# Constant products on TensorE around the norms, and a convolution norm moved into the attention, in a three-layer transformer kernel

## Chip, cores and metric

One core of one Trainium2 chip runs the whole program in one launch. The metric is the device time of one execution in microseconds; of the kernel before it is the median of three runs.

## The reference

512 tokens of width 1024 pass through two equal layers (first block), then one different layer (second block), all in float32.

- First block, twice: `x = LN(a*x + 0.5*swiglu(x))`, hidden width 2816; `x = LN(a*x + mix)`; the same FFN form again with other weights. The mixer projects `x` to queries and keys of two attentions: one with latent queries and keys (8 heads, 64 + 32 rotary columns), one sparse attention (8 heads, 2 key groups, window, selected and compressed keys). Rotary tables are `cos` and `sin` of position. Two sigmoid-gated projections are added and projected once more.
- Second block: `x = x + mix(rms(x)) @ w_out`, then a mixture of 16 experts with top-2 routing. The mix is the concatenation of three parts:

```
o_gla  = gated linear attention (4 heads of 64), rms norm per head, times silu(out_gate)
y      = causal depthwise conv (width 31) of a * sigmoid(g)          # 256 channels
yn     = group norm of y over 64 channels, * gain + bias;  o_conv = yn * sigmoid(yn)
o_diff = (softmax(q1 k1^T) - lam * softmax(q2 k2^T)) v, rms norm per head of 128, gain
mix    = concat(o_gla, o_conv, o_diff);  x = x + mix @ w_out
```

## The kernel before

**Layout.** Activations lie transposed: 8 tiles of 128 features by 512 tokens (`xa`). Each float32 product is made of three in a faster format: an operand is split into a high and a low part (`xhi`, `xlo`; `whi`, `wlo`), and TensorE adds high x low, low x high and high x high in one bank. A weight block is 128 output features: 24 matmuls of 128x512. SyncE loads it into `raw` (two slots), ScalarE rounds it to `whi` (line 569), GpSimd subtracts for `wlo` (line 2631); `whi`/`wlo` have four slots, freed in order by `w_free`. Each engine runs its instructions in program order; the order is written out by hand, with semaphores between engines. `sync_point` (line 393) is a barrier between stages: TensorE and ScalarE raise `at_sync`, VectorE waits for both, clears the local semaphores and lets them go.

**First block.** `pe_ffn` (line 483) computes the FFN. Its first two tiles run interleaved, following the norm tile by tile (`pe_first_pair`, line 465): for each `k` four matmuls on `xhi[k]`, two on `xlo[k]`. The down projection has 8 output tiles of two blocks of 11 (66 matmuls). VectorE adds a finished tile to the residual (line 675) and accumulates sums in `zs` and squares in `sq_sum`; the last tile's sums come separately. `pe_stats` (line 516) turns these into per-token statistics with matmuls of one column (line 520, `sums`), then spreads the reciprocal roots over a bank (`pe_spread`, line 551, transposes). `dve_stats` (line 729) computes in between. Then comes `sync_point`, then the norm: VectorE, ScalarE (`xhi`) and GpSimd (`xlo`) tile by tile. After the FFN follow `pe_mixer` (line 1035), a barrier, `pe_mixer_out` (line 1152: MLA units with gate products as filler, projections), `pe_stats`, and the second FFN. Between the two layers VectorE frees the banks for the next FFN only after its norm.

At the start of the mixer ScalarE issues five DMAs (lines 1191 to 1197): two of the rotary tables `rope`, two of `w1`, one of `vbd`. All add to `cmp_dma`. `rope` lies in memory that the FFN's `hlo` occupies. VectorE waits for all five (line 1316) before tile 0's rotation (`rotate`, line 1305: multiply, shuffle at line 1309, which frees the bank). TensorE waits for them at the compression.

**Second block.** `pe_squares` (line 536) sums squares by pairs of tiles for the first norm. `pe_second` (line 1591) runs 19 input tiles with the linear attention's levels and the convolution taps (60 on VectorE) beside them, then 32 attention units (`pe_units_whole`, line 793; 4 heads x 2 maps x 4 query tiles; 128 to 512 keys). Unit `u` on TensorE: filler (`pe_late`), scores of `u`, transposes of unit `u - 2`, values of `u - 3`. `act_units` and `dve_units` call `act_late` and `dve_late` after each unit in the same way. The filler is four late projection tiles, six matmuls a unit over units 0 to 15 (24 in all for each), then the rest of the linear attention; the output gates are made of `Exp` (ScalarE, units 20, 21), add and reciprocal (VectorE, unit 22). `finish_dif` (line 2226) combines eight groups of four units.

After the last unit: VectorE squares and reduces the attention's output (lines 2252, 2254) for the per-head norm, ScalarE takes the root, VectorE scales all of it (line 2262), TensorE transposes 16 blocks (line 1651). The conv norm runs beside it: means by `blk64` (line 1642), subtraction (2258), squares (1978), variance (1646), root (1981), reciprocal of 128x1024 (2265), gain, bias, sigmoid (1986), product (2276). `split_mix` (line 2103) writes each mix tile's high and low part; heads follow one by one. `mix_ready` counts tiles. TensorE waits for all eight, then runs the eight tiles of `w_out`, one after the other in two banks, with `pe_pair_sums` for the next norm among them. Router, gather and 23 expert blocks follow.

## Time and profile before

| | us |
|---|---|
| median of 3 runs (3226.43 to 3226.77) | 3226.52 |
| profiled execution | 3226.44 |
| its span | 3224.6 |
| TensorE busy | 2927.3 (91%) |
| VectorE busy | 1526.1 (47%) |
| ScalarE busy | 1216.3 (38%) |
| GpSimd busy | 1167.2 (36%) |

The mean granted TensorE clock is 0.949 of full speed. Times in the trace count from the first instruction. Engines are PE (TensorE matmul), PEld (its weight loads), DVE (VectorE), ACT (ScalarE), POOL (GpSimd), SP (SyncE). In a timeline a row is a start, a duration, engine, line and operation, and in brackets how long the engine was idle before and which engine's work ended that. A matmul of two fp32 operands is two records.

### The profile page before, as it was taken

What the parts mean: (1) busy time and instruction counts of PE and PEld (TensorE: products, weight loads), DVE (VectorE), ACT (ScalarE), POOL (GpSimd) and SP (SyncE); (2) the same over time, 40 slices, a digit from 0 to 9 for tenths busy, and PEclk for the clock granted to TensorE, in tenths of its full rate; (3) what the DMA queues carried; (4) which work ended last, traced back from release to release, by engine and by line L of the source; (5) the groups of instructions that cost most, each with busy time, mean ns of one, the idle gap of its engine ahead of it and who ended that gap; (6) DMA issues with size and microseconds to landing.
All of it is one profiled execution on the core that took longest, in us unless ns stands there. A gap on an engine that the chain in (4) does not pass through costs nothing.

```text
span 3224.6 us, 38218 instructions
## 1 busy us (share of the span) xinstructions
PE 2927.3 (91%) x13393; PEld 2335.0 (72%) x13393; DVE 1526.1 (47%) x2594; ACT 1216.3 (38%) x1854; POOL 1167.2 (36%) x602
## 2 busy tenths in 40 slices
PE   6999989988999998999989998999999797866997
PEld 5887777657778876887868756778878676655665
DVE  4441364445744314433154544663332577555665
ACT  3332233555343323333132465443332342424553
POOL 3444342421444443444443341244444342011221
PEclk9999999999999998999989999999999798978998
DMA  3333232202323331333232211323332121014996
GB/s 127 94 96 104 78 121 71 64 17 67 123 85 97 97 99 61 91 98 106 94 104 79 86 30 33 110 76 105 92 105 96 36 79 46 20 65 150 358 354 208
DMA packets 118547, 324.19 MB, mean 101 GB/s; under 512 B 12432, under 2 KB 48656, under 8 KB 117904
## 3 DMA queue, kind: packets, MB, share of 16 engines
q1 hardware_dynamic: 108992, 305.17, 29.6%
q10 hardware_dynamic: 2800, 8.91, 0.7%
q0 software_dynamic: 6624, 8.41, 0.7%
q8 instruction: 77, 1.26, 0.2%
q14 instruction: 54, 0.44, 0.0%
HBM read 313.52 MB, written 24.64 MB: 105 GB/s over the span
## 4 chain that ended last, share of the span: by engine, by line
PE 63%; issue 15%; DVE 10%; POOL 7%; ACT 4%; DMA 2%; POOLq 0%; DVEq 0%; ACTq 0%; SPq 0%; another core or an unknown queue 0%
PE ps L417 14%; PE ps L418 14%; PE ps L420 14%; POOL wlo L2631 6%; PE ps L452 3%; PE ps L1910 2%; PE ps L929 2%; PE ps L1896 1%; PE ps L1898 1%; PE ps L1897 1%; DVE cacc L2178 1%; PE ps L827 1%; PE ps L1739 1%; PE ps L1882 1%; ACT xhi L646 1%
## 5 line engine op out<-in xcount | busy, mean ns | idle before, releaser
L2631 POOL TENSOR_TENSOR wlo<-raw,whi 128x1024 fp32r<-128x1024 f32 (+1 forms) x368 | 953.4, 2592 | 1580.2 <-ACT whi L569 1580.2
L417 PE MATMUL ps<-xlo,whi 128*128 128x512 f32 x1736 | 683.7, 394 | 40.8 <-DVE xlo L2107 19.2
L569 ACT ACTIVATE whi<-raw 128x1024 fp32r<-128x1024 f32 (+1 forms) x368 | 409.1, 1112 | 820.8 <-PE ps L420 779.6
L418 PE MATMUL ps<-xhi,wlo 128*128 128x512 f32 x1736 | 680.5, 392 | 0.0
L420 PE MATMUL ps<-xhi,whi 128*128 128x512 f32 x1736 | 428.7, 389 | 0.0
L417 PEld LDWEIGHTS ps<-xlo,whi 128*128 128x128 f32 x1736 | 329.6, 190 | 113.1 <-issue 21.7
L418 PEld LDWEIGHTS ps<-xhi,wlo 128*128 128x128 f32 x1736 | 329.2, 190 | 67.9
L420 PEld LDWEIGHTS ps<-xhi,whi 128*128 128x128 f32 x1736 | 325.9, 188 | 67.7
L417 PE MATMUL ps<-hlo,whi 128*128 128x512 f32 x704 | 281.4, 400 | 10.0 <-DVE hlo L664 10.0
L418 PE MATMUL ps<-hhi,wlo 128*128 128x512 f32 x704 | 279.3, 397 | 0.0
L675 DVE SCALAR_TENSOR_TENSOR xa<-ps,xa 128x512 f32<-128x512 f32 x48 | 33.1, 690 | 405.5 <-PE ps L420 405.5
L659 DVE TENSOR_TENSOR sg<-sg,ps 128x512 f32<-128x512 f32 x88 | 60.6, 688 | 346.8 <-PE ps L420 346.1
L664 DVE TENSOR_TENSOR hlo<-sg,hhi 128x512 f32 x88 | 213.2, 2422 | 10.8
L592 ACT ACTIVATE sg<-ps 128x512 f32<-128x512 f32 x88 | 52.8, 600 | 334.0 <-PE ps L420 312.0
L420 PE MATMUL ps<-hhi,whi 128*128 128x512 f32 x704 | 171.5, 391 | 0.0
L417 PEld LDWEIGHTS ps<-hlo,whi 128*128 128x128 f32 x704 | 134.5, 191 | 42.1 <-issue 12.7
L656 DVE TENSOR_TENSOR sg<-sg,ps 128x512 f32<-128x512 f32 x88 | 60.5, 688 | 215.6 <-ACT sg L592 215.6
L418 PEld LDWEIGHTS ps<-hhi,wlo 128*128 128x128 f32 x704 | 134.5, 191 | 30.5 <-issue 1.0
L420 PEld LDWEIGHTS ps<-hhi,whi 128*128 128x128 f32 x704 | 132.2, 188 | 29.0
L2431 DVE TENSOR_TENSOR mlo<-mraw,mhi 128x2048 fp32r<-128x2048 f32 x46 | 103.3, 2288 | 49.8 <-ACT mhi L2060 49.6
L452 PE MATMUL ps<-xlo,whi 128*128 128x512 f32 x256 | 116.5, 455 | 8.7 <-DVEq L397 4.6
L452 PE MATMUL ps<-xhi,wlo 128*128 128x512 f32 x256 | 108.6, 424 | 0.0
(569 smaller groups left out, 4729.6 us busy)
## 6 DMA issues: line engine op xcount, KB each, us to landing
raw<-in_gu SPq DMA_DIRECT2D x176, 512.0 KB, 3.6
raw<-in_mix SPq DMA_DIRECT2D x96, 512.0 KB, 3.7
mraw<-in_w SPq DMA_DIRECT2D x23, 2048.0 KB, 12.3
raw<-in_dn SPq DMA_DIRECT2D x64, 704.0 KB, 4.0
mdraw<-in_w SPq DMA_DIRECT2D x23, 1024.0 KB, 13.4
raw<-in_w SPq DMA_DIRECT2D x32, 512.0 KB, 3.6
gate_rows<-tails SPq DMA_DIRECT2D x32, 256.0 KB, 4.3
sgmn<-gate_rows SPq DMA_DIRECT2D x16, 512.0 KB, 4.3
```

Of the source, the lines that this page charges most:

```text
L417: nc.tensor.matmul(out, whi[:, slot, cols], rlo, start=first and t == 0, stop=False)
L418: nc.tensor.matmul(out, wlo[:, slot, cols], rhi, start=False, stop=False)
L420: ins = nc.tensor.matmul(out, whi[:, slot, kk * P:kk * P + P], rhi, start=False, stop=last and t == n - 1)
L452: ins = nc.tensor.matmul(out, w[:, slot, t * P:t * P + P], x[:, t, :], start=k == 0, stop=k == 3 * KT - 1)
L569: nc.scalar.activation(whi[:, s, 0:n], raw[:, r, 0:n], ACT.Copy).then_inc(hi_done, 1)
L656: nc.vector.tensor_tensor(sg[:, j, :], sg[:, j, :], ps[0][:], ALU.mult).then_inc(S["tile_free"], 1)
L659: nc.vector.tensor_tensor(sg[:, j, :], sg[:, j, :], ps[1][:], ALU.mult).then_inc(S["tile_free"], 1)
L664: nc.vector.tensor_tensor(hlo[:, bass.ds(i * 2 + j, 1), :], sg[:, j:j + 1, :], hhi[:, bass.ds(i * 2 + j, 1), :].bitcast(F32), ALU.subtract ...
L929: ins = nc.tensor.matmul(bank[:], v_keys[:, br, kt, :], p_group[G % 2][:, kt, :, :].rearrange("p j q -> p (j q)"), start=br == 0 and kt == ...
L1910: ins = nc.tensor.matmul(ps[2 + half][:].rearrange("p (n c) -> p n c", n=4), hT[b % 2][:, j, :], mdraw[b % 3][:, 4 * half:4 * half + 4, j, ...
L2431: nc.vector.tensor_tensor(mlo[b % 2][:, :, k], mraw[b % 2][:, :, k], mhi[b % 2][:, :, k].bitcast(F32), ALU.subtract).then_inc(m_lo, 1)
L2631: nc.gpsimd.tensor_tensor(wlo[:, s, 0:n], raw[:, r, 0:n], whi[:, s, 0:n].bitcast(F32), ALU.subtract).then_inc(w_ready, 1)
```

## The change

1. `rope` gets a semaphore of its own and is issued by ScalarE before the barrier that ends the first FFN; `cmp_dma` thresholds fall by 32.
2. The sums of `zs` and `sq_sum` move out of `pe_stats` into the last tile: between its two blocks in the FFN, between its low passes and its high pass in the mixer.
3. `pe_idle(n)` issues `n` products of the identity and a 128x256 constant into a bank that nothing reads. They stand in `sync_point` after TensorE's increment (5 after each `pe_stats`, 8 between mixer and mixer output, 9 and 2 in the second block), in `pe_stats` (2 and 1), in `pe_squares` (24, then 1 after each of four pairs), after the last two pair sums (2 and 1) and before the experts' gather (10).
4. The conv norm's statistics, roots, reciprocal (eight pieces), gain and bias move into units 0 to 15 of the attention; the late tiles run eight matmuls a unit over units 4 to 15; conv and output gates use one `Sigmoid` group at unit 20. `finish_dif` reduces squares by group; heads are scaled one by one; `w_out` tiles 0 to 3 run together in four banks, by mix tile.

```diff
+    def pe_idle(n, bank=None):
+        for _ in range(n):
+            nc.tensor.matmul((bank or ps[5])[:, 0:256], ident, c("maskc")[:, 0:256], start=True, stop=True)
@@ sync_point(eng, who, idle=0)
             eng.sem_inc(S["at_sync"], 1)
+            pe_idle(idle)
             eng.wait_ge(go, 1)
@@ products(..., between=None)
             nc.tensor.matmul(out, wlo[:, slot, cols], rhi, start=False, stop=False)
+        if between:
+            between()
@@ down(i, mm), in pe_ffn
+                if b == 0 and mm == KT - 1:
+                    pe_early_sums(pe)
@@
+    def pe_early_sums(pe):
         pe.wait_ge(S["own2"], 11)
         sums(ps[4], 0, zs[:])
         pe.wait_ge(S["pair_ready"], 6)
         sums(ps[4], 4, sq_sum).then_inc(S["pair_used"], 1)
+    def pe_stats(pe, t0):
+        pe_idle(2)
         pe.wait_ge(S["tile_free"], t0 + 2 + KT)
         sums(ps[2], 0, xa[:, KT - 1, :]).then_inc(S["pair_used"], 1)
         pe.wait_ge(S["squared"], KT)
         sums(ps[3], 0, sq_one).then_inc(S["pair_used"], 1)
+        pe_idle(1)
...
@@ pe_mixer_out
+                       between=(lambda: pe_early_sums(pe)) if j == KT - 1 else None)
@@ dve_mixer
-        dve.wait_ge(S["cmp_dma"], 80)
+        dve.wait_ge(rope_in, L * 32 + 32)
@@ pe_second, after the units
-        pe.wait_ge(S["own_cq"], 1)
-        for k in range(2):
-            ins = nc.tensor.matmul(ps[k][:], c("blk64"), cacc[:, k, :], start=True, stop=True)
...
+        for b in range(4):
+            pe.wait_ge(w_ready, B2 * G_LAYER + (G2_OUT + b + 1 + 2))
+        pe.wait_ge(S["mix_ready"], 4)
+        for k in (2, 3):
+            pe_four_tiles(pe, k)
         for h in range(4):
+            pe.wait_ge(S["gl_ready"], h + 1)
             for qt in range(QT):
                 ins = nc.tensor.transpose(ps[4 + h][:, qt * P:(qt + 1) * P], o_dif[:, qt, h * P:(h + 1) * P], ident)
             ins.then_inc(S["aux_ready"], 1)
+            if 1 <= h <= 2:
+                pe_four_tiles(pe, h - 1)
+        for k in range(4, KT):
+            pe.wait_ge(S["mix_ready"], k + 1)
+            pe_four_tiles(pe, k)
+        for j in range(4, KT):
+            pe_x_block(pe, B2, G2_OUT, 0, j, j % 4, j - 1)
...
@@ pe_four_tiles(pe, k): for b in range(4), ps[b] += three products of mix tile k
@@ pe_late
+        if u == 0:
+            for k in range(2):
+                ins = nc.tensor.matmul(ps[k][:], c("blk64"), cacc[:, k, :], start=True, stop=True)
+            ins.then_inc(S["stat_ready"], 1)
+        if u == 2:
+            for k in range(2):
+                pe.wait_ge(S["sq_ready"], k + 1)
+                nc.tensor.matmul(ps[k][:], c("blk64"), rs2[:, k, :], start=True, stop=True).then_inc(S["stat_used"], 1)
+        n, k0 = divmod(u - LATE_AT, LATE_UNITS)      # LATE_AT, LATE_UNITS = 4, 3; before 0, 4
+                if n < 2:
+                    pe.wait_ge(S["std_ready"], n + 1)
@@ act_late
+            for k in range(2):                        # u == 1
+                act.wait_ge(S["norm_dve"], k + 1)
+                nc.scalar.activation(rs2[:, k, :], cacc[:, k, :], ACT.Square).then_inc(S["sq_ready"], 1)
+        if u == 3:
+            for k in range(2):
+                act.wait_ge(S["stat_used"], k + 1)
+                nc.scalar.activation(rs2[:, k, :], ps[k][:], ACT.Sqrt, bias=eps_ap(RMS_EPS)).then_inc(S["std_ready"], 1)
+        if u == OG_AT:
+                nc.scalar.activation(og_sig[:, half, :], og[half][:], ACT.Sigmoid).then_inc(S["og_exp"], 1)
+            nc.scalar.activation(conv_sig[:], cacc[:], ACT.Sigmoid).then_inc(S["sig_ready"], 1)
@@ dve_late
-            own.link(nc.vector.tensor_scalar(og_sig[:], og_sig[:], 1.0, None, ALU.add))
-            own.link(nc.vector.reciprocal(og_sig[:], og_sig[:]))
+        if u == 1: ...                                # cacc -= mean, two 128x512
+        if 5 <= u < 13:
+            r = rs2[:, (u - 5) // 4, (u - 5) % 4 * P:(u - 5) % 4 * P + P]
+            own.link(nc.vector.reciprocal(r, r))
+        if u == 13: ...                               # gain;  u == 14: bias
+        if u == OG_AT + 3: ...                        # cacc *= conv_sig, 128x1024
+        if u in (OG_AT + 5, OG_AT + 7): ...           # split_mix of conv tiles 2 and 3
@@ finish_dif
+            for h in range(2):
+                own.link(nc.vector.tensor_tensor_reduce(sg[:, 0, 256 + P * h:256 + P * h + P], o[:, h, :], o[:, h, :], 1.0,
+                                                       0.0, ALU.mult, ALU.add, rt3[:, r:r + 1]))
@@ act, first layer loop, after act_ffn and act_root
+            for k in range(2):
+                act.dma_start(rope[:, 2 * k:2 * k + 2, :], ...).then_inc(rope_in, 16)
             sync_point(act, "act")
```

## Rows read from the trace of the kernel before

**Rows 1.** TensorE's waits, all: who for whom, total us, times, longest
```profile
PE ps L417 <- DVE xlo L2107: 19.2, 1, 19.2
PE ps L417 <- DVE sg L1309: 17.0, 4, 8.4
PE ps L547 <- DVE squares L769: 16.3, 3, 14.6
```
**Rows 2.** Stretches, second block: length, busy us by engine, clock, DMA share, GB/s
```profile
2724.00:2764.00 40.00, 39.72 (x204) 29.46 (x204) 12.26 (x59) 19.24 (x52) 9.52 (x4) 1.00 0.18 53
2764.00:2784.00 20.00, 16.95 (x100) 12.84 (x100) 10.68 (x38) 11.36 (x29) 0.00 (x0) 1.00 0.00 1
2784.00:2803.00 19.00, 11.41 (x51) 10.15 (x51) 11.12 (x15) 2.46 (x6) 0.00 (x0) 0.64 0.00 1
2803.00:2826.00 23.00, 20.87 (x141) 16.77 (x140) 17.64 (x43) 13.57 (x26) 0.00 (x0) 1.00 0.00 1
2826.00:2864.00 38.00, 10.24 (x27) 5.17 (x25) 31.04 (x34) 8.85 (x11) 2.43 (x1) 0.54 0.05 14
2864.00:2913.00 49.00, 48.67 (x213) 40.37 (x213) 7.36 (x12) 9.17 (x12) 12.35 (x5) 0.94 0.29 97
```
**Rows 3.** Short stretches at either clock: PE, PEld, DVE, ACT, POOL, clock
```profile
404.30:409.10 4.80, 4.80 (x11) 3.41 (x12) 4.80 (x8) 4.80 (x8) 4.12 (x4) 0.50 0.00 0
409.60:417.50 7.90, 7.90 (x36) 6.54 (x35) 2.99 (x5) 6.70 (x9) 7.21 (x6) 1.00 0.50 177
425.40:429.40 4.00, 3.98 (x9) 3.13 (x10) 3.86 (x3) 0.14 (x1) 2.60 (x1) 0.50 0.02 9
709.60:713.80 4.20, 4.15 (x15) 3.67 (x16) 1.61 (x7) 2.28 (x6) 0.00 (x0) 0.58 0.00 0
1969.90:1976.90 7.00, 7.00 (x22) 5.92 (x23) 3.38 (x12) 4.59 (x11) 0.00 (x0) 0.56 0.00 0
2563.90:2577.60 13.70, 13.70 (x48) 10.96 (x48) 11.18 (x21) 5.25 (x8) 7.55 (x5) 0.78 0.01 1
```
**Rows 4.** Timeline, start of the mixer, layer 0
```profile
417.76 0.59 ACT L1202 ACTIVATE g_t<-ps 24x512 f32<-24x512 f32 x1 [0.55 <-PE ps L479]
...
423.93 0.69 DVE L1308 TENSOR_TENSOR k_pe<-ps,rope 32x512 f32<-32x512 f32 x1 [11.20 <-DMA vbd<-in_zero]
...
424.55 0.72 DVE L1309 STREAM_SHUFFLE sg<-ps 32x512 f32<-32x512 f32 x1
...
425.42 0.77 PE L417 MATMUL ps<-xlo,whi 128*128 128x512 f32 x1 [7.47 <-DVE sg L1309]
```
**Rows 5.** Timeline, end of the first FFN, layer 0
```profile
394.89 0.95 PE L520 MATMUL ps<-con,zs 128*128 128x1 f32 x8
...
395.09 0.69 DVE L675 SCALAR_TENSOR_TENSOR xa<-ps,xa 128x512 f32<-128x512 f32 x1 [10.88 <-PE ps L420]
...
396.59 1.03 PE L520 MATMUL ps<-con,xa 128*128 128x1 f32 x8
...
404.26 0.79 PE L475 MATMUL ps<-xhi,whi 128*128 128x512 f32 x1 [2.92 <-ACT xhi L646]
```
**Rows 6.** Timeline, end of the mixer, layer 0
```profile
886.30 1.05 PE L520 MATMUL ps<-con,zs 128*128 128x1 f32 x8 [0.23 <-DVE zs L719]
```
**Rows 7.** Timeline, attention of the second block; last, a line of groups
```profile
2776.69 1.56 PE L1753 MATMUL ps<-vT,k_rows 128*128 128x256 f32 x6 [2.30 <-ACT vT L1789]
...
2784.37 6.55 DVE L1807 RECIPROCAL og_sig<-og_sig 128x1024 f32<-128x1024 f32 x1
...
2816.23 1.28 ACT L1796 ACT_TABLE_LOAD   x1
...
2817.53 0.31 ACT L1796 ACTIVATE small<-small 128x16 f32<-128x16 f32 x1
...
L861 DVE CUSTOM_DVE_ANT_0 s_sb<-ps,con 128x128 f32<-128x128 f32 (+3 forms) x66 | 32.4, 491 | 84.5 <-PE ps L808 83.6
```
**Rows 8.** Timeline, before the MLA units, layer 0
```profile
705.77 0.47 PE L452 MATMUL ps<-xlo,whi 128*128 128x512 f32 x1 [2.30 <-DVEq L397]
```

More of the change, by code:

```diff
@@ L402, in sync_point, with products @@
             eng.sem_inc(S["at_sync"], 1)
+            pe_idle(idle)
             eng.wait_ge(go, 1)
             eng.sem_clear(go)
-    def products(out, parts, first=True, last=True, ready=None):
+    def products(out, parts, first=True, last=True, ready=None, between=None):
         n = len(parts)
@@ L422, in products, with pe_x_block @@
         return ins
-    def pe_x_block(pe, L, g, i, j, bank, free, ver=None, x=(xhi, xlo), ready=None):
+    def pe_x_block(pe, L, g, i, j, bank, free, ver=None, x=(xhi, xlo), ready=None, between=None):
         pe.wait_ge(w_ready, L * G_LAYER + i * 4 + (g + j + 1 + 2))
@@ L514, in pe_shift, with sums @@
         nc.tensor.matmul(ps[2][:], c("ones"), zs[:], start=True, stop=True).then_inc(S["stat_ready"], 1)
-    def pe_stats(pe, t0):
-        def sums(bank, c0, x):
-            for qt in range(QT):
-                ins = nc.tensor.matmul(bank[:, c0 + qt:c0 + qt + 1], x[:, qt * P:(qt + 1) * P], c("ones")[:, 0:1],
-                                       start=True, stop=True)
-            return ins
+    def sums(bank, c0, x):
+        for qt in range(QT):
+            ins = nc.tensor.matmul(bank[:, c0 + qt:c0 + qt + 1], x[:, qt * P:(qt + 1) * P], c("ones")[:, 0:1],
+                                   start=True, stop=True)
+        return ins
+    def pe_early_sums(pe):
         pe.wait_ge(S["own2"], 11)
@@ L1790, in act_late @@
                                      ACT.Copy).then_inc(S["v_rows"], 1)
-            if u == OG_AT + half:
+        if u == OG_AT:
+            for half in range(2):
                 act.wait_ge(S["late_out"], 3 + half)
-                nc.scalar.activation(og_sig[:, half, :], og[half][:], ACT.Exp, scale=-1.0).then_inc(S["og_exp"], 1)
+                nc.scalar.activation(og_sig[:, half, :], og[half][:], ACT.Sigmoid).then_inc(S["og_exp"], 1)
+            act.wait_ge(S["own_cq"], 1)
+            nc.scalar.activation(conv_sig[:], cacc[:], ACT.Sigmoid).then_inc(S["sig_ready"], 1)
         if u == GLA_AT + 4:
@@ L2250, in dve_second @@
-        flat = o_dif[:].rearrange("p q (h v) -> p (q h) v", v=P)
-        sq = sqd[:].rearrange("p q (h v) -> p (q h) v", v=P)
-        own.link(nc.vector.tensor_tensor(sq, flat, flat, ALU.mult))
-        own.wait()
-        nc.vector.tensor_reduce(rt2, sq, AX_X, ALU.add).then_inc(S["gel_ready"], 1)
-        dve.wait_ge(S["stat_ready"], 1)
-        for k in range(2):
-            nc.vector.tensor_tensor(cacc[:, k, :], cacc[:, k, :], ps[k][:], ALU.subtract).then_inc(S["norm_dve"], 1)
-        dve.wait_ge(S["gel_ready"], 2)
@@ L2260, in dve_second @@
-        own.link(nc.vector.reciprocal(rt2, rt2))
-        own.wait()
-        nc.vector.tensor_tensor(flat, flat, rt2.unsqueeze(2).broadcast_to([P, 16, P]),
-                                ALU.mult).then_inc(S["gl_ready"], 1)
-        dve.wait_ge(S["std_ready"], 2)
-        own.link(nc.vector.reciprocal(rs2[:], rs2[:]))
-        own.wait()
-        for k in range(2):
-            own.link(nc.vector.scalar_tensor_tensor(out=cacc[:, k, :], in0=cacc[:, k, :], scalar=p2("cng", k),
-                                                   in1=rs2[:, k, :], op0=ALU.mult, op1=ALU.mult))
@@ L2270, in dve_second, with scaled @@
-        own.wait()
-        for k in range(2):
-            own.link(nc.vector.tensor_scalar(cacc[:, k, :], cacc[:, k, :], p2("cnb", k), None, ALU.add))
-        own.wait()
-        dve.sem_inc(S["own_cq"], 1)
-        dve.wait_ge(S["sig_ready"], 1)
-        own.link(nc.vector.tensor_tensor(cacc[:], cacc[:], rs2[:], ALU.mult))
-        own.wait()
-        for k in range(2):
-            split_mix(dve, own, 2 + k, cacc[:, k, :])
+        dve.sem_inc(S["gel_ready"], 1)
+        def scaled(h):
+            o = o_dif[:, :, h * P:(h + 1) * P]
+            r = rt3.rearrange("p (q h) -> p q h", h=4)[:, :, h:h + 1].broadcast_to([P, QT, P])
+            nc.vector.tensor_tensor(o, o, r, ALU.mult).then_inc(S["gl_ready"], 1)
@@ L2280, in dve_second @@
+        dve.wait_ge(S["gel_ready"], 2)
+        own.link(nc.vector.reciprocal(rt3, rt3))
+        own.wait()
+        scaled(0)
+        scaled(1)
         for h in range(4):
@@ L2831, in _ @@
             act_root(act, LN_EPS)
+            for k in range(2):
+                act.dma_start(rope[:, 2 * k:2 * k + 2, :], d["rope"].rearrange("k p t -> p k t")
+                              [:, 2 * k:2 * k + 2, :]).then_inc(rope_in, 16)
             sync_point(act, "act")
```

133 lines of the change are left out of this document (75 added, 58 removed).

## The prediction

> **What bounds the kernel now.** I read the totals first: TensorE is busy 91% of the span, so a microsecond is won only where TensorE stands still or runs at the low clock. The list of TensorE's waits then says where it stands still [rows 1]: 19.2 us once, ahead of the second block's output projection; two stretches of about 8 us behind a VectorE shuffle (line 1309); 14.6 us ahead of the second block's first norm. The table of stretches shows what stands around the longest [rows 2]: from 2826 to 2864 TensorE is busy 10.24 of 38 us and VectorE 31.04, so VectorE's serial chain of sub-layer norms is the bound there; from 2784 to 2803 TensorE has 11.41 of 19 us at a mean clock of 0.64. The table of short stretches gives the price of the clock [rows 3]: after a norm the granted clock is 0.50 (1.2 GHz) and 11 records take 4.80 us, 0.436 each; later it is 1.00 (2.4 GHz) and 36 take 7.90, 0.219 each. The reader is to see that a slow stretch costs only where TensorE is the bound, and then half of its length.
>
> **Part 1, rope tables early.** The first rotation of each layer waits 11.20 us for DMAs, and what it waits for last is the fifth transfer in ScalarE's queue, two weight tables of 1 MB among the five [rows 4]. Tile 2 of the mixer needs the bank that this rotation frees, so TensorE stands 7.47 us in layer 0 and 8.4 in layer 1 [rows 1, 4]. With the tables issued before the norm and only they awaited, the wait is over long before 412. What is late next is the ordinary chain: gate sigmoid 0.59, rotation 0.69, shuffle 0.72, and the handoffs, some 2.3 us for each layer. ScalarE's two issues stand beside VectorE's two scalings after the statistics (1.4 us, two passes at L675's 0.69 [rows 5]) and are hidden; uncovered they would cost under 1 us each layer. The compression waits for its weights much later. Gain: 7.5 + 8.4 - 2 x 2.3 = 11.3 us. The slow 4.0 us after the wait (9 records, clock 0.50) [rows 3] go as well, 2 us each, unless the new 2.3 us gap drops the clock; I take half. **-13.3**, bounds -15 and -9.
>
> **Part 2, early sums.** Now the sixteen one-column products for `zs` and `sq_sum` follow the last tile (from 394.89), beside VectorE's add (395.09, 0.69), and the sums of `xa` start at 396.59 [rows 5]. Moved into the last tile, they cost TensorE the same 1.9 us, but nothing covers the add any more: it now ends 0.95 us after a tile that itself ends 1.9 us later, where before the sums of `xa` started 1.55 us after the tile. The chain is 1.9 + 0.95 - 1.55 = 1.3 later; I take 1.15, since the `squared` wait hides a little. Four FFN boundaries: +4.6. In the mixer it is worse: there the sums stand behind the low passes of one 5.5 us tile, which end at 884.1, while `zs` is ready only at 886.3 [rows 6], so TensorE stalls 2.2 us with eight matmuls behind the wait. Two boundaries at 2.8: +5.6. Bounds for the part: 0 (if the products slip between matmuls) and +12.
>
> **Part 3, idle products.** No row shows a 128x256 constant product; the nearest is L1753, fp32 with 256 columns, six records (three products) in 1.56 us at full clock [rows 7]: 0.47 to 0.52 us each, about twice that at the low one. Five fill 2.4 of the 2.92 us ahead of the next norm's first tile [rows 5]; 5 + 24 take 14 us of the 14.6 [rows 1]; nine 4.3 of 4.8. All fit if the clock is full when they start, and it is, since dense tiles precede. What they buy, with each after-norm pair of tiles held at 48 records: TensorE needs 11 us, but the low half arrives every 1.3 us and paces it at 12.2, against 13.7 now. So a pair gains 1.1 to 1.5 us, not the 2.4 that the clock alone gives: -5.5 for four. The broadcast transposes gain 0.45 at each of six: -2.7. Between the two layers TensorE waits 14 us with five idles, so that restart stays slow: 0. The second block's squares gain 2.1 in their four-step ping-pong and its pair 1.6 (clock 0.78 over 13.7 us [rows 3]): -3.7. With part 2: **-1.7**, bounds -6 and +14. The upper one: clock falls regardless, nothing is gained, each idle group overhangs its gap by 1 us.
>
> The eight idles before the MLA units fill the wait of 2.30 us [rows 8] and the 2.7 behind it; the gate feed slips 1.2 us inside that gap, at no cost. Behind it 4.2 us run at clock 0.58 in layer 0 and 7.0 at 0.56 in layer 1 [rows 3], TensorE busy throughout: half of each, 5.6. **-5**, bounds -6 and +2. The remaining idles (router, gather) sit in gaps and win about **-1**.
>
> **Part 4, second block.** Tail: from the last attention product (2826.2) to the last tile of the projection (2912.6) pass 86.4 us. After: norm statistics are gathered unit by unit, the conv result is ready, and TensorE starts on rows 2 and 3 of the first four tiles (24 matmuls, 5.5 us) while VectorE scales head 0. I walked the heads: each costs VectorE about 2.6 us (scaling, gain, split in two) and each group of 12 matmuls costs TensorE 2.7, so TensorE never waits. It needs 192 matmuls at 0.228 (213 records in 48.67 us [rows 2]) 43.8, 16 transposes 1.8, sums 1.9, and one gap: slots of the first four tiles come free together at the end, so tile 4 waits for ScalarE's and GpSimd's conversion, 1.75. Together 49.2: -37.2. Bounds -40 and -30.
>
> Attention: the statistics of the conv norm stand at units 0 and 2, and late tile 0 waits at unit 4 for ScalarE's roots. With TensorE in order, squares (after VectorE's two subtractions) hold it till 2730.3 and the roots with their table load till 2736.9, where unit 4 now begins at 2732.9: +4.0. The late tiles lose four units of overlap: 24 of 96 matmuls move onto units 4 to 15, +5.5. The two holes of 3.5 and 2.6 us may cost clock: +2. Against it, VectorE's add and reciprocal of the output gates (6.55 us at 2784.37 [rows 7]), which hold the softmax chain and then the clock through the recurrent products (0.64 [rows 2]), become one sigmoid: unit 25's scores come 11.9 us earlier, less 1.4 for ScalarE's 4.9 us of sigmoids and tables at unit 20: -10.5. The cost of the same reciprocal in eight pieces is hidden: VectorE has 12.26 of 40 us in those units. In units 25 to 31 it has 17.64 of 23 us [rows 2]; two splits (under 1.4 each, two passes of 0.69) and four reductions (nearest form, L861, 0.49 [rows 7]) make it the bound: +2.5. Sum **+3.5**, bounds -6 and +14.
>
> ScalarE here takes two switch pairs more. The row: a load takes 1.28 and its activation begins 0.02 later, 2816.23 to 2817.53 [rows 7]; I used that. The Trainium skill, page "ScalarE: Activation LUTs", section "What ACT_TABLE_LOAD costs", adds a drain of about 1.38 us to each switch, 2.66 in all. By that rule the four loads would cost 5.5 us more on ScalarE and the sum would be 3177; the row shows no such time behind the load or ahead of it.
>
> **Sum.** -13.3 - 1.7 - 5 - 1 - 37.2 + 3.5 = -54.7. The profiled execution took 3226.44 us (span 3224.6); so 3171.7. The median of the three runs, 3226.52, is 0.1 above it.
>
> **Rivals.**
> 1. The attention becomes latency-bound: VectorE's and ScalarE's queued norm work delays the softmax chain in every unit. For: two engines in order, ten inserted waits. Against: VectorE is busy under a third of units 0 to 15 [rows 2]. It would take part 4's attention to its +14, and the tail to -32: 3171.7 + 10.5 + 5 = 3187.
> 2. The clock does not hold: low activity around the one-column products drops it as now, and idles run at double length. For: the clock falls now while TensorE is still issuing such products. Against: dense idles stand before, between and behind them. Parts 2 and 3 at their upper ends, +14 and +2 in place of -1.7 and -5, give 3194; with half of the places failing, 3183.
> 3. The clock gives more: stretches that now fall by chance of a 2.5 us gap do not fall. For: the falls at gaps of that size come and go in this trace. 3159.
> 4. The tables' drain as a mechanism of this kernel: ScalarE stands 1.4 us more at each of four switches in the attention, all reaching TensorE: 3177. Only the page speaks for it.
> 5. Slower: idle products are real work in TensorE's order, 116 of them. If most waits that they should fill have gone and the clock stays low, each costs its full 1 us: +116 against -55 - 3. It decides from 55 of them exposed at the low clock, where the sum's gain is spent; at 70, 3171.7 + 70 = 3242. Against: the waits of 14.6 [rows 1], 2.92 [rows 5] and 2.30 us [rows 8] stand in the rows and nothing in the change removes them.
> 6. The change does not do what it says: the conv norm in the attention saves nothing since head norms alone hold VectorE as long. They are four of 2.6 us against TensorE's 2.7, so this needs them doubled: tail -15, 3194.
>
> **How the numbers follow.** Forecast 0.50; rival 1 0.14; 2 0.12; 3 0.12; 4 0.04; 5 0.03; 6 0.05. The likeliest is 3171.7. Its own range, from half of each part's bounds added as independent, is 3163 to 3180. The range reaches to rivals 1, 2 and 3 and leaves out 5 and 6: 3154 to 3190. Faster by over 0.2% (6.5 us, about what a measurement of this kernel tells from none) in every case but 5 and a part of 6: 0.96; within 0.2% 0.015; slower 0.025.
>
> **What would show it.** Right: the 19.2 us wait is gone, TensorE is busy over 90% from the attention's end, with one gap near 1.8 us ahead of tile 4; the shuffle waits are near 2 us; a stall of 2 us stands inside the last output tile of both mixers; the clock is 1.00 through five norms and low between the layers; TensorE has two holes in units 0 to 4. Wrong: the clock at 0.50 behind the idles; VectorE ahead of TensorE's waits in the projection; a saving outside 37 to 73 us.

## The result, and the profile after

The changed kernel took 3193.02 us (median of four, 3181.23 to 3199.03), 0.9887 of the kernel before, 95% interval 0.9872 to 0.9902: 1.1% faster, where 3171.7 was forecast and the range ended at 3190. The sign held, the size did not: 33.5 us instead of 54.7, by medians. Ten times of the changed kernel in two sets lie between 3181.2 and 3199.6; the lowest two have a granted clock of 0.970 and 0.971 and the highest two 0.964 and 0.965. The kernel before, near 3226.5 in its first times, spread as widely when it was run eleven times beside the experiments (3220.8 to 3236.7). So differences of a few microseconds are read from traces below, and from medians only above some 8 us.

The profiled execution took 3188.26 us (span 3186.2). Its page, the line of busy times and the granted clock by slices:

```profile
PE 2961.5 (93%) x13625; PEld 2361.4 (74%) x13625; DVE 1525.9 (48%) x2632; ACT 1217.9 (38%) x1856; POOL 1173.6 (37%) x602
...
PEclk9999999999999999999999999999999998999998
```

TensorE's waits in the second block, from 2640 to 2890 us (who waits for whom, total, times, longest), answer to [rows 1] and [rows 2]: the 19.2 us behind the split is gone; new are the two waits at L1768 and L1783, in the first units of the attention. The first line, in the router, stood before too, with 15.2 us.

```profile
PE ps L1938 <- DVE k_wide L2281: 18.3, 1, 18.3
...
PE ps L1768 <- ACT rs L1826: 3.7, 1, 3.7
PE ps L1783 <- ACT rs L1830: 2.5, 1, 2.5
...
PE ps L425 <- POOL wlo L2684: 1.6, 1, 1.6
```

Three stretches of the same block: length, busy us of PE, PEld, DVE, ACT, POOL, clock, DMA share, GB/s. The second and third are the output stage: TensorE has 56.9 of 59 us, where [rows 2] had 10.24 of 38. The first is the price at the attention's start: TensorE is busy all the time, at 0.50.

```profile
2729.00:2739.00 10.00, 9.60 (x26) 6.96 (x27) 0.51 (x3) 2.86 (x6) 0.00 (x0) 0.50 0.00 0
...
2822.00:2864.00 42.00, 40.37 (x208) 34.27 (x208) 23.96 (x46) 10.24 (x16) 9.97 (x4) 0.97 0.14 38
2864.00:2881.00 17.00, 16.53 (x86) 13.89 (x85) 3.78 (x6) 3.48 (x5) 2.40 (x1) 1.00 0.50 187
```

**The account.** Each product of TensorE in one trace has its like in the other. The difference of their start times is taken ahead of a step and behind it; by how much it moved is what the step cost. So the whole difference divides (us, against the trace of the kernel before; the last column is a second trace of the same changed kernel):

```
step                                        forecast   first trace  second trace
rotary tables, two layers                     -13.3       -13.6        -11.8
mixer's end to second FFN, layer 0             +1.0        +4.0         +4.8
mixer's end to second FFN, layer 1             +1.0        +4.2         +2.8
first FFN's end to mixer, both layers          -1.4        -1.2         -1.3
FFN's end to next layer                        +0.7        +1.3         +1.3
FFN's end to the second block's tiles          -3.0        -1.7         -3.0
MLA units                                      -5          -4.6         -4.2
attention, from before it to its last product  +3.5       +12.2        +12.0
output stage                                  -37.2       -37.2        -37.2
all else (router, clock falls by chance)       -1          -1.6         -6.1
sum                                           -54.7       -38.2        -42.7
```

A row changes by 1.5 or 3 us where the clock fell once more or less. One row can change by much more, since it rests on a single trace of the kernel before: its attention, from its first product to its last, took 101.7 us there, and 110.5 in the trace of a kernel whose second block is the same ("Rotary tables alone" below). The mean granted clock over it was 0.93 in the one and 0.81 in the other. The changed kernel's 113.1, in both its traces, is 11.5 above the one and 2.7 above the other. So the +12 of that row is sure only against this one trace. The forecast's rows 2 to 6 are its -1.7, put where its terms belong: two mixers at 2.8, four FFN boundaries at 1.15, less the pairs', transposes' and squares' gains.

### The profile page after: what moved, and what is told of

It reads as the page before. It is cut to its first block, busy times and chain, and to the rows that moved or that the text cites. A ratio compares the mean times of both kernels' runs of the same rounds, so it can differ in the third digit from the quotient of the medians.

```text
span 3186.2 us, 38726 instructions
## 1 busy us (share of the span) xinstructions
PE 2961.5 (93%) x13625; PEld 2361.4 (74%) x13625; DVE 1525.9 (48%) x2632; ACT 1217.9 (38%) x1856; POOL 1173.6 (37%) x602
## 4 chain that ended last, share of the span: by engine, by line
PE 40%; issue 32%; POOL 14%; DVE 9%; ACT 3%; DMA 1%; POOLq 0%; SPq 0%; DVEq 0%; ACTq 0%; another core or an unknown queue 0%
POOL wlo L2684 13%; PE ps L430 6%; PE ps L425 6%; PE ps L426 6%; PE ps L462 3%; PE ps L1988 2%; PE ps L950 2%; PE ps L1974 1%; PE ps L1976 1%; PE ps L1975 1%; DVE cacc L2246 1%; PE ps L848 1%; PE ps L1783 1%; POOL xlo L808 1%; PE ps L1960 1%
## 5 line engine op out<-in xcount | busy, mean ns | idle before, releaser
L425 PE MATMUL ps<-xlo,whi 128*128 128x512 f32 x1704 | 668.0, 392 | 13.7 <-DVE sg L677 6.4
L426 PE MATMUL ps<-xhi,wlo 128*128 128x512 f32 x1704 | 665.0, 390 | 0.0
L430 PE MATMUL ps<-xhi,whi 128*128 128x512 f32 x1704 | 420.8, 389 | 0.0
L425 PEld LDWEIGHTS ps<-xlo,whi 128*128 128x128 f32 x1704 | 321.2, 189 | 84.9 <-POOL wlo L2684 11.4
L426 PEld LDWEIGHTS ps<-xhi,wlo 128*128 128x128 f32 x1704 | 321.1, 188 | 66.0
L685 DVE TENSOR_TENSOR hlo<-sg,hhi 128x512 f32 x88 | 213.1, 2422 | 10.8
L462 PE MATMUL ps<-xlo,whi 128*128 128x512 f32 x256 | 114.6, 448 | 4.1 <-DVE o_nsa L1463 4.1
L462 PE MATMUL ps<-xhi,wlo 128*128 128x512 f32 x256 | 106.5, 416 | 0.0
```

The source lines that it names most:

```text
L425: nc.tensor.matmul(out, whi[:, slot, cols], rlo, start=first and t == 0, stop=False)
L426: nc.tensor.matmul(out, wlo[:, slot, cols], rhi, start=False, stop=False)
L430: ins = nc.tensor.matmul(out, whi[:, slot, kk * P:kk * P + P], rhi, start=False, stop=last and t == n - 1)
L462: ins = nc.tensor.matmul(out, w[:, slot, t * P:t * P + P], x[:, t, :], start=k == 0, stop=k == 3 * KT - 1)
L685: nc.vector.tensor_tensor(hlo[:, bass.ds(i * 2 + j, 1), :], sg[:, j:j + 1, :], hhi[:, bass.ds(i * 2 + j, 1), :].bitcast(F32), ALU.subtract ...
```

## The experiments

**The changed kernel again.** No edit.

> The changed kernel once more, unedited, for a second trace and more times. Its four times so far spread from 3181 to 3199 us (granted clock 0.970 and 0.965), while the kernel before stays near 3226.5. Theory: the low-clock stretches fall differently from run to run, since the changed kernel leaves many gaps of 2 to 4 us that sometimes drop the clock; so the times spread again by over 10 us around 3190, a low time goes with a high granted clock, and work outside the low-clock stretches takes the same time as in the first trace. Rival: the spread was chance of the chip on that day; then five times lie within 3 us of each other.

3187.47 us (3183.61 to 3199.55). The theory held: the same spread, and a high clock with a low time. Its column stands above: the two traces of one kernel differ by clock falls, and by some 1.5 us in each of two down projections (see the end).

**The mixers' sums late.**

```diff
-                       between=(lambda: pe_early_sums(pe)) if j == KT - 1 else None)
+                       between=None)
...
-        pe_idle(2)
+        if not early:
+            pe_early_sums(pe)
+        else:
+            pe_idle(2)
```

> The early sums are undone in the two mixers alone (they follow the last tile again, and the two idle products ahead of them go); the four FFN boundaries keep theirs. Theory: in the last output tile of each mixer TensorE waits 2.02 us for the sum zs, which VectorE shares with GpSimd's weight work, and this stall also drops the clock, so that the eight high products after it take 3.65 us in place of 2.00; with the sums behind the tile both go, and the first norm product of each mixer comes 3 to 4 us earlier: 6 to 8 us in all, about 3186 against 3193. Rival 1: only the stall goes and the clock falls a little later instead, 4 us in all. Rival 2: the loss at the mixers comes from the restart behind the norm, not from the sums: within 1 us of the changed kernel.

The median, 3188.98 (3170.14 to 3192.48), shows no gain over the changed kernel's 3187.47. The profiled execution is the fastest of the five by 16 us, so what follows is read from single steps of its trace, not from its time. Mixer's end in the changed kernel, layer 0, TensorE's and VectorE's rows (start, us, line, tiles, count, idle before and its releaser):

```profile
874.65 2.15 DVE L740 TENSOR_TENSOR zs<-zs,xa 128x512 f32<-128x512 f32 x1
...
876.85 1.05 PE L531 MATMUL ps<-con,zs 128*128 128x1 f32 x8 [2.02 <-DVE zs L740]
877.76 1.04 PE L531 MATMUL ps<-con,sg 128*128 128x1 f32 x8
878.67 3.65 PE L430 MATMUL ps<-yhi,whi 128*128 128x512 f32 x8
...
890.40 0.50 PE L485 MATMUL ps<-xhi,whi 128*128 128x512 f32 x1 [1.18 <-ACT xhi L667]
```

and with the sums behind the tile:

```profile
876.41 2.00 PE L430 MATMUL ps<-yhi,whi 128*128 128x512 f32 x8
878.62 1.05 PE L531 MATMUL ps<-con,zs 128*128 128x1 f32 x8 [0.21 <-DVE zs L743]
...
887.85 0.58 PE L485 MATMUL ps<-xhi,whi 128*128 128x512 f32 x1
```

In the first, TensorE stands 2.02 us and the eight high products take 3.65 us instead of 2.00. The sums take their 1.8 us in either place, but behind the tile they cover VectorE's last add; here idle products (0.94 us) stand beside it instead, where only 0.21 were spent: 2.02 + 1.65 + 0.73 = 4.4. From the last low product to the sums of `xa` pass 8.65 to 10.21 us in all twelve such places of the six traces with the sums inside the tile, and 4.24 to 4.27 in every trace with the sums behind it, the kernel before among them. The larger values come where the clock falls among the sums already (the second group of them takes 1.85 us instead of 1.03 in layer 1 of the first trace). Against the kernel before, the step up to the norm's first tiles is now -1.0 us in layer 0 and -1.2 in layer 1 instead of the two traces' means of +4.4 and +3.5: 5.4 and 4.7 us won. The theory's 3 to 4 us for each mixer was too low, since it left out the add and the earlier falls.

Two things about the cause. The sum is late because the add to `zs` (L740) takes 2.15 us beside a GpSimd pass over weights; the same add takes 0.69 in the four FFNs, where no such pass runs beside it. And the one-column products alone don't bring the clock down: the same early sums, without a stall, stand between dense products at the four FFN boundaries, and in all 24 such places of the six traces they take 1.7 us and the clock stays. The first of them:

```profile
386.34 0.95 PE L531 MATMUL ps<-con,zs 128*128 128x1 f32 x8
387.15 1.03 PE L531 MATMUL ps<-con,sg 128*128 128x1 f32 x8
388.04 0.48 PE L425 MATMUL ps<-hlo,whi 128*128 128x512 f32 x1
```

Whether the stall would do it here without such products behind it is not shown: no run has it that way in this place, and behind the 2.0 us waits at tile 2 of the mixers, where none stand, the clock fell in some traces and not in others.

**No idle products.** `pe_idle` returns at once.

> All products on constants are taken out, nothing else. Theory: they work where a dense stretch precedes them and the gap is short: they won about 1.4 us at the first FFN boundary, some 4 us at the two starts of the MLA units and 1.7 us at the second block's first norm, and cost next to nothing where they win nothing; without them the kernel is 8 to 14 us slower, about 3203. Rival 1 (the forecast's size: 16 us of clock gains): 3209. Rival 2: the idle products are exposed or useless in most places: not slower than 3193.

3198.27 us (3185.77 to 3201.86), 10.8 above the changed kernel in the same set (5.3 above its first median), near the theory, though the intervals of the two ratios overlap (0.9877 to 0.9917, and 0.9862 to 0.9901). In its trace the MLA units of layer 1 gain nothing (0.1 us in place of -3.8 and -4.0), the second block's start nothing (in place of -1.7 and -3.0), the first FFN's end 0.1 (in place of -0.8). So the idle products do win in these places. Their sum, about 11 us where the forecast's terms together held 18, rests on the medians and is loose.

**One bank for the norm's statistics.** The sums go through bank 1 one at a time (units 0, 1, 3, 4); late tile 0 runs in bank 0 over units 0 to 3, the others from unit 6.

```diff
+        if u < 4:
+            return 0, 6 * u, 6
+        n, k0 = divmod(u - 6, 3)
+        return (n + 1, 8 * k0, 8) if u >= 6 else (-1, 1, 0)
...
+            nc.tensor.matmul(ps[1][:], c("blk64"), cacc[:, u, :], start=True, stop=True).then_inc(S["stat_ready"], 1)
```

> The statistics of the convolution's norm in the attention take one bank instead of two, one product at a time (units 0, 1, 3, 4), so that the first late projection tile runs in the other bank over units 0 to 3 as it did in the kernel before; the other three follow from unit 6 on, eight products a unit. The computation is the same. Theory: what made the attention's start 18 us worse than in the kernel before (the forecast had 11.5) is that TensorE has nothing to do over units 0 to 3 but wait for the squares (3.7 us) and the roots (2.5 us), that the clock falls there and stays low for 10 us, and that 24 products wait till unit 4; with late products between them both holes go and the attention ends 10 to 14 us earlier, about 3181. Rival 1: the softmax chain through VectorE and ScalarE, with the norm's work queued in it, sets the pace of every unit: at most 3 us are won. Rival 2: only the clock goes back, not the order: 5 us.

3188.39 us (3187.32 to 3194.93): the theory failed, nothing was won. The first units of the attention in the changed kernel, then two rows of this one, a wait of TensorE from 2764 to 2812 us and a stretch:

```profile
2714.93 1.98 PE L1763 MATMUL ps<-cacc,con 128*128 128x512 f32 x4 [1.87 <-DVEq L404]
...
2721.11 3.09 PE L1768 MATMUL ps<-rs,con 128*128 128x512 f32 x4 [3.71 <-ACT rs L1826]
...
2729.40 0.77 PE L1783 MATMUL ps<-xlo,whi 128*128 128x512 f32 x1 [2.46 <-ACT rs L1830]
```
```profile
PE ps L848 <- ACT pt L868: 4.1, 1, 4.1
```
```profile
2773.00:2804.00 31.00, 30.31 (x106) 24.15 (x107) 13.82 (x47) 15.06 (x32) 0.00 (x0) 0.51 0.03 13
```

The start did gain: unit 16's first score product comes 54.4 us after the attention's first product instead of 56.8. But holes of 1.5 and 3.1 us remained, with 17 us of low clock from the first of them on, and then the clock fell once more, at 2773, and stayed low for 30 us: units 22 to 24 took 3.37 us each, in the changed kernel 1.87, 3.40 and 1.87.

**Idle products in the two holes.**

```diff
         if u == 2:
+            pe_idle(7, ps[7])
             for k in range(2):
...
+        if u == 4:
+            pe_idle(5, ps[7])
```

> Idle products are added in the two places of the attention's start where TensorE waits: seven ahead of unit 2's wait for the squares (3.71 us), five ahead of unit 4's wait for the roots (2.46 us); one takes 0.46 us at the full clock in the changed kernel's trace. Theory: the low clock that begins in the first hole costs the squares' products 1.1 us (3.09 in place of 1.98) and units 2 to 6 some 5 us (unit 4 to 5 takes 7.74 and 5.08 where a unit with eight late products at the full clock takes 2.82); with the holes filled the clock stays, and unit 16 comes 5 to 6 us earlier after unit 0 than its 54.87 us. Rival 1: the clock falls in spite of the idle products: nothing is won, or 1 us lost where they overhang. Rival 2: ScalarE and VectorE hold units 2 to 6 anyway: under 2 us. In the time of the whole this is near what one set of rounds can tell, so the trace's units decide.

3179.38 us (3177.32 to 3183.34), 8.1 below the changed kernel's 3187.47, with intervals that overlap a little (0.9835 to 0.9874, and 0.9862 to 0.9901). The products that took 3.09 us, and the stretch behind them that ran at 0.50:

```profile
2716.12 1.98 PE L1769 MATMUL ps<-rs,con 128*128 128x512 f32 x4 [0.49 <-ACT rs L1829]
```
```profile
2718.00:2730.00 12.00, 11.40 (x56) 8.72 (x56) 2.91 (x13) 6.81 (x16) 0.00 (x0) 1.00 0.14 43
```

Unit 16 comes 48.98 us after unit 0 instead of 54.87: 5.9 us, as the theory had it. The effect goes on: the 10 us at 0.50 near the attention's end are down to some 3, and from its first product to its last pass 105.0 us instead of 113.1. The output stage then has a new gap of 1.27 us at its start and takes 50.6 us instead of 49.4. In three other traces with the holes unfilled ("All sums late", "Long idle" and the last experiment) the clock fell at other moments and unit 16 came 53.2 to 53.3 us after unit 0, so what the holes cost in clock is 4.3 us there.

**All sums late.** As the mixers' case, at the FFN boundaries too.

> The early sums are undone at all six boundaries (they follow the last tile again), and the two idle products ahead of the last tile's sums go with them; one idle stays ahead of the transposes. The run with only the mixers' sums late won 5.4 us at each mixer in its trace. Theory: at the mixers again 5 us each; at the four FFN boundaries, where the sums are ready in time and cost only their own 1.9 us uncovered, 1.2 us each, if the clock holds up to the norm: 15 us in all against the changed kernel's trace, 4 to 5 us better than with the mixers' alone. Rival: with the early sums' work gone from before and the idles gone from beside the last add, the clock falls around the one-column products at the FFN boundaries, the transposes take 1.97 us again in place of 1.09 and the first norm pair runs slow: worse by 1 to 2 us at each FFN boundary than the changed kernel.

3172.65 us (3169.45 to 3177.30), 14.8 below the changed kernel, and the intervals of the ratios don't overlap (0.9813 to 0.9847). The theory's 15 us came, but not in its places: at the FFN boundaries the trace shows -0.9, +1.3, -1.1 and -1.9 us, the changed kernel -0.8, +1.3, -0.4 and -1.7 to -3.0. The sums' 1.2 us were won and mostly given to the clock, by the rival's mechanism, though its loss of 1 to 2 us at each boundary did not come. The mixers' steps are won as before (4.27 and 4.26 us from the last low product to the sums of `xa`). Where the rest of the 14.8 us lies isn't shown: with the mixers' sums alone late the median was 3188.98, 16 us above this one, while the pair of kernels below that differ in the same way are 0.1 us apart. The transposes of the first one, here and in the changed kernel:

```profile
401.17 1.97 PE L573 MATMUL ps<-con,small 128*128 128x128 f32 x8
```
```profile
399.46 1.09 PE L575 MATMUL ps<-con,small 128*128 128x128 f32 x8 [0.32 <-DVE small L766]
```

**Rotary tables alone**, on the kernel before.

> The kernel before with the one edit that ScalarE issues the rotary tables ahead of the norm and VectorE waits for them alone. Theory: the wait of 7.5 and 8.4 us at tile 2 of each mixer becomes one of about 2 us, and the low clock behind it goes: 13 to 14 us, so 3213 against 3226.5, and in the trace the offset to the kernel before moves by 6 to 7.5 us between the norm and tile 3 of each mixer and nowhere else. Rival 1: the tables come late in their new place too, since they share the queue with the blocks of weights: under 8 us. Rival 2: the low clock of the norm's first pair now reaches further into the mixer and takes 2 us of each back: 10 us.

3211.92 us (3205.21 to 3218.89) against 3228.19 in the same set, ratio 0.9950 (0.9932 to 0.9968). In the trace the step is -7.6 us in layer 0 and -7.4 in layer 1, and the end -14.6. So the theory's steps came; its "nowhere else" did not. The offset moved by up to 5 us in other places too, where the code is that of before, and back by 8.8 in the attention. The wait that was 7.47 us [rows 4], and the stretch of the attention at the low clock that the trace of before doesn't have at this length:

```profile
419.04 0.47 PE L418 MATMUL ps<-xlo,whi 128*128 128x512 f32 x1 [1.98 <-DVE sg L1307]
```
```profile
2757.00:2794.00 37.00, 32.87 (x116) 26.34 (x115) 17.94 (x34) 7.98 (x19) 0.00 (x0) 0.50 0.00 1
```

**Long idle between the layers.**

```diff
-            sync_point(pe, "pe", 5)
+            sync_point(pe, "pe", 28)
```

> The changed kernel with 28 idle products in place of five between the layers, where TensorE waits 11 to 14 us for VectorE's norm, and 1 in place of 24 at the second block's start (the two follow each other, so that place keeps its number). Theory: at the restart between the layers the clock is 0.50 now and the first pair of tiles takes as long as before; with the wait filled it stays at 1.00, and the restart is 1.3 to 2.5 us earlier; nothing else moves. Rival 1: the idles run at the low clock from the start (they begin as it falls, at 1268 us), take 0.9 us each, overhang the wait by 10 us and the kernel is 10 us slower. Rival 2: no difference, since the low half of the norm's tiles, one each 1.3 us, paces the pair at either clock.

3182.84 us (3177.68 to 3192.55), not to be told from the changed kernel. The idles end 3 us short of the restart, and it runs at 0.50 as before:

```profile
1267.85 12.25 PE L398 MATMUL ps<-con 128*128 128x256 f32 x56
1283.07 0.79 PE L485 MATMUL ps<-xhi,whi 128*128 128x512 f32 x1 [2.97 <-DVEq L747]
```

**Put together.** Mixers' sums late, the holes filled, 34 idles between the layers.

> Three edits of the runs before put together: the mixers' sums late, idle products in the two holes of the attention's start, and 34 idle products in place of 28 between the layers. In the run with 28 they ended at 1280.1 us, TensorE then waited 2.97 us and the clock fell at 1282; six more take 2.6 us and reach to the restart. Theory: 10 us from the two mixers, 6 from the holes and 2 from the restart, off the changed kernel's 3187.5 of the first set of rounds: 3169, and the granted clock through the restart at 1283 stays at 1.00. Rival 1: the gains don't add, because each saved wait moves the places where the clock falls: 3177. Rival 2: at the restart the clock falls again although the wait is filled, and 34 idles overhang: 2 us worse than with 28 there.

3167.04 us (3164.81 to 3174.02), ratio 0.9815 (0.9796 to 0.9835): 20 us below the changed kernel of the first set of rounds, and the intervals of the ratios don't touch. It beats both kernels and is 2 us from the theory's 3169; rival 1 (3177) is out. At the restart the wait is filled and the first product takes 0.49 us, not 0.79:

```profile
1264.48 16.17 PE L398 MATMUL ps<-con 128*128 128x256 f32 x68
1281.11 0.49 PE L485 MATMUL ps<-xhi,whi 128*128 128x512 f32 x1 [0.46 <-issue]
```

That step costs +0.8 us here against +1.3: 0.5 us of the 2 that the theory had for it.

**The same with the FFNs' sums late too.**

> As the first kernel of this set, with the sums late at the FFN boundaries too. In the run with all sums late the FFN boundaries came out level with early ones: 1.2 us were saved on the sums and lost again, as the clock fell at 399 us and the transposes took 1.97 us instead of 1.09. Theory: the same as the first kernel within 2 us. Rival: the run with all sums late was the fastest of its set, 3172.7 against 3189 with the mixers' alone late, so late sums at the FFN boundaries are worth several microseconds that one trace each didn't show: 3165 or less, 4 us or more ahead of the first kernel.

3167.17 us (3164.20 to 3168.80): the same within 0.2 us, as the theory said. At the FFN boundaries, where the sums' inputs are ready in time, these runs show no difference between early and late sums.

**One bank again**, with its holes filled and the gain and bias two units later.

> As the first kernel of this set, with the one-bank order of the attention's start in place of the two-bank one: first late tile over units 0 to 3, idle products in its two remaining holes (three ahead of unit 4's product, six ahead of unit 6), and the gain and bias of the convolution's norm two and more units later (16 and 17 in place of 14 and 15), where they don't meet the combination of a group at unit 15. Theory: the one-bank order lost because TensorE stood 4.1 us at unit 17 behind VectorE (gain, bias and a group's combination with a squares pass of 2.42 us in a row) and the clock then stayed low for 30 us; with both causes gone, unit 16 comes 43 to 46 us after unit 0 (49.0 with the holes filled in the two-bank order) and the whole is 3 to 6 us ahead of the first kernel. Rival: with the late products ended at unit 14, units 15 to 24 are too thin to hold the clock whatever VectorE does; it falls again near unit 18 and the kernel is 8 us or more behind the first.

3177.65 us (3171.30 to 3183.13), 10.6 behind. Unit 16 came 46.8 us after unit 0, 2.2 ahead of the first kernel's 49.0, the 4.1 us wait was gone, and the clock fell again at 2759. This kernel, then the first one, over the same stretch:

```profile
2759.00:2801.00 42.00, 41.51 (x148) 33.26 (x146) 17.12 (x55) 16.21 (x34) 0.00 (x0) 0.51 0.00 1
```
```profile
2759.00:2801.00 42.00, 36.79 (x222) 29.40 (x220) 28.47 (x87) 24.20 (x46) 0.00 (x0) 0.92 0.02 8
```

The rival held in its outcome. Whether what decides is that the late products end at unit 14 rather than 15 wasn't tried by itself and stays open.

**The second block's edits alone**, on the kernel before, without idle products.

> The change's edits of the second block alone, on the kernel before: no idle products, no early sums, rotary tables where they were. Theory: the time goes by the two stages as in the changed kernel's traces: the output stage 37 us shorter, the attention from its start to its last product 12 to 13 us longer, together 25 us: 3202. Before the second block nothing moves. Rival 1 (the forecast's terms, attention 3.5 us longer): 3193. Rival 2: without idle products the attention starts on a low clock and loses 5 us more: 3207.

3193.99 us (3190.86 to 3207.33) against 3227.35, ratio 0.9906 (0.9885 to 0.9927), so 24 to 37 us. In the trace the two stages give -25.1 us, the theory's number; another 10 us went before the second block, where the code is that of before: clock falls that the one trace of before has (for one at 2659 to 2666 us) and this one has not. By the time of the whole it is rival 1's 3193 that came, and not the theory's 3202. Since the attention of the code of before took 101.7 us in one trace and 110.5 in another, these runs can't tell whether the edits lengthen it by 12 us or by 3.5 in the mean.

## Why the prediction missed

**Right.** The tables (-13.3 forecast; -13.6 and -11.8 in the two traces, -15.0 by the edit alone; behind the 2 us wait the clock fell in the second trace and not in the first, which is the half that the forecast took); the shuffle wait is 2.0 us. The output stage: -37.2 was forecast and measured, 86.5 to 49.4 us, with one gap ahead of tile 4 (1.75 forecast, 1.6 measured). The heads' norms never held TensorE there, so rival 6 is out. The gates: from unit 20 to unit 26 pass 21.9 us instead of 32.5, 10.6 less (10.5 forecast; in part luck, since in the other trace with the old code these units took 37.5 us). The 2 us stall in the last tile of both mixers stands at its place and size (2.2 forecast; 2.02 and 2.00). Rival 5 is out: without the idle products the kernel is slower, not faster. So is rival 4. ScalarE at the roots, in the changed kernel:

```profile
2727.00 0.26 ACT L868 ACTIVATE pt<-ps 128x128 f32<-128x128 f32 x1
2727.27 1.28 ACT L1830 ACT_TABLE_LOAD   x1
2728.57 1.27 ACT L1830 ACTIVATE rs<-ps,small 128x512 f32<-128x512 f32 x2
```

The load follows its forerunner by 0.01 us and its activation follows it by 0.02. The Trainium skill, page "ScalarE: Activation LUTs", section "What ACT_TABLE_LOAD costs", would have 1.38 us of drain here; this case's traces show none, and the measurement decides.

**Wrong, first: "Two boundaries at 2.8: +5.6" and "the clock is 1.00 through five norms".** Undoing the mixers' early sums won 5.4 and 4.7 us, 10.1 in all, where 5.6 was booked. The stall was foreseen at its size, but the term priced it as a wait alone, and what the clock would do behind it was put at nothing. The high products behind it ran at 0.50 and took 1.4 to 1.8 us longer each time (3.65, 3.76, 3.76 and 3.39 instead of 2.00), in some places the sums and idle products too, and 0.7 us of VectorE's add came uncovered. Nor was the clock 1.00 through five norms: in the first trace it was at the first of them, and 0.87 to 0.91 in the mean over the other four; in the second trace it was at four, and 0.90 over the second block's. This is half of rival 2, by another path: the one-column products between dense ones left the clock alone at the FFN boundaries, and with the stall ahead of them it fell in every mixer. (The prediction counts sixteen such products; they are eight, two records each, and the times it uses are right.)

**Wrong, second: "The two holes of 3.5 and 2.6 us may cost clock: +2".** The holes were forecast at 3.5 and 2.6 us and came at 3.7 and 2.5, their position too. The clock behind them cost 5.9 us up to unit 16, not 2: it fell within 1 us of the first hole's end, came back for some 3 us, and fell again in the second; the sixteen late products and the scores of units 4 and 5 ran at 0.50 till 2739. Besides this, unit 16 came 1.6 us later than 4.0 + 5.5 and the clock make it (56.8 us after the start of the stage, 39.8 before), and units 25 to 31 at +4.6 instead of +2.5, with 10 us at 0.50 from 2814. Attention in all: +12 where +3.5 was forecast, against the one trace of before. That is near rival 1's size (+14), but not its cause: filling the holes alone brought 8.1 us of it back, 105.0 us against 101.7, which is the forecast's +3.5 nearly to the point. So the terms for the work itself were sound together, and the clock behind the holes was the term that was mis-sized.

**Wrong, third: the idle products' gains.** 18 us of clock were booked in part 3; without the idles the kernel loses 10.8, by medians whose intervals overlap. Which of its places fell short isn't settled beyond the rows above.

**How it adds up.** Against -54.7, the traces give -38.2 and -42.7: mixers +6.2 and +5.6 off the forecast, attention +8.7 and +8.5, second block's start +1.3 and 0, layer boundary +0.6 twice. What is left beyond these is clock falls of 1.5 to 3 us that come and go between two executions of one program; a range that was built from the terms' bounds alone had no room for them. The attention's share of the miss, +8.7 and +8.5, has the trace of before as its other side: against the other trace of the old second block it would be nearly nothing, and other rows would carry the difference. What stands apart from that choice is what the experiments took away again: 10.1 us at the mixers, 8.1 at the holes.

## What to carry to other kernels

When an edit puts a wait into a dense run of products, price it as the wait plus what the low clock may take from the products behind it: here 2.0 + 1.4 to 1.8 us in the mixer, 6.2 us of holes + 4.3 to 5.9 at the attention's start. The same edit was free where its input was ready (the FFN boundaries), and cost 4 to 6 us where VectorE made the input beside GpSimd's weight work. Fillers that ended half a microsecond ahead of the restart kept its clock at 1.00 (16.2 us of them); fillers that ended three short did not (12.3 us: 0.50). In the one-bank kernels, work moved into earlier holes won at the start and the clock fell later for longer; that the one made the other isn't shown. And before a stage's cost is booked against one trace, see what a second trace of the same code takes there: here 101.7 and 110.5 us.

## What the runs showed that was not expected

- The time at the low clock fell far more than the number of its stretches: stretches at 0.50 before the last one sum to 307 us in the trace of before (31 of them), 167 in the changed kernel (29), 130 in the best version (29). Times follow: 3226, 3188, 3166 in the same executions.
- A stall of 2.02 us between dense products was followed by products at 1.2 GHz in both mixers and both traces; waits of 2.0 us at tile 2 of the mixer were followed by a fall in some traces and by none in others. What tells them apart was not settled.
- In the first trace two of the four down projections ran 1.2% slower at the full clock (0.2317 us between products in the mean, in place of 0.2290; 1.4 to 1.6 us each); in the second trace none did. Three traces of the experiments have one or two such ("One bank", "All sums late" and the last one), at other places. The cause is open.
